# Head-pair scan of a hybrid RWKV-7 / PEER layer: score products over zero-padded 128-row operands, two PSUM banks for scores, and one barrier between passes

## The reference, cut to what matters

```python
def step(s, xs):                      # s: state [value, key] of one head
    r_t, w_t, k_t, v_t, kk_t, a_t = xs
    sa = jnp.einsum('bhvk,bhk->bhv', s, -kk_t)
    s = (s * w_t[:, :, None, :] + sa[..., None] * (kk_t * a_t)[:, :, None, :]
         + v_t[..., None] * k_t[:, :, None, :])
    y = jnp.einsum('bhvk,bhk->bhv', s, r_t)
```

## Time and profile before

| what | us |
| --- | --- |
| median of 3 runs | 3511.05 |
| lowest, highest | 3495.39, 3520.24 |
| profiled execution, its own time | 3520.24 |
| its span in the profile | 3518.1 |
| the scan's block, 808.5 to 1381.7 | 573.2 |
| mean granted TensorE clock in the scan | 0.95 |

### The profile page before, as it was taken

How to read it: one execution, slowest core, us unless ns; L and a number is a source line. 1 busy time by engine, 2 the same in 40 slices (tenths; PEclk the granted TensorE clock), 3 DMA queues, 4 the chain that set the end, 5 groups by cost and what they waited for, 6 DMA issues and landing times.

```text
span 3518.1 us, 58248 instructions
## 1 busy us (share of the span) xinstructions
PE 3053.6 (87%) x22248; PEld 2615.1 (74%) x22248; DVE 2436.1 (69%) x3113; ACT 1434.1 (41%) x1827; POOL 726.0 (21%) x386
## 2 busy tenths in 40 slices
PE   6987998967888887696997877699999799999997
PEld 2336998955666665685997877699999687787776
DVE  5995553247555655535998877577777698999997
ACT  6884332323333334225333555433333243333333
POOL 0000000001010001103664322111111234444442
PEclk9998999987999999898998988899999899999998
DMA  9992332300000000223445888899999999999996
GB/s 378 421 406 108 120 130 106 122 23 5 8 5 5 5 7 26 83 84 147 141 153 194 299 300 300 292 346 358 360 359 356 402 418 417 417 417 417 417 417 258
DMA packets 207434, 811.63 MB, mean 231 GB/s; under 512 B 81472, under 2 KB 101056, under 8 KB 118336
## 3 DMA queue, kind: packets, MB, share of 16 engines
q1 hardware_dynamic: 170432, 541.14, 41.4%
q0 software_dynamic: 36864, 268.45, 19.1%
HBM read 769.16 MB, written 40.37 MB: 230 GB/s over the span
## 4 chain that ended last, share of the span: by engine, by line
DMA 27%; PE 11%; DVE 9%; ACT 4%; issue 3%; SPq 1%; POOL 1%; DVEq 0%; ACTq 0%
DMA work<-act_table 12%; DMA raw<-expert_u 11%; DMA x<-u_rows,idx 3%; DVE wlo L2076 2%; ACT whi L1733 2%; DVE x L2034 2%; DVE wlo L2116 2%; PE ps L1538 1%; PE ps L1539 1%; PE ps L1540 1%; PE ps L1795 1%; PE ps L1796 1%; PE ps L1797 1%; DVE wlo L1527 1%; DVE work L2111 1%
## 5 line engine op out<-in xcount | busy, mean ns | idle before, releaser
L1538 PE MATMUL ps<-hhi,whi 128*128 128x256 f32 x2048 | 595.9, 291 | 68.8 <-DVE wlo L1527 31.5
L1539 PE MATMUL ps<-hlo,whi 128*128 128x256 f32 x2048 | 584.8, 286 | 0.0
L1540 PE MATMUL ps<-hhi,wlo 128*128 128x256 f32 x2048 | 584.4, 285 | 0.0
L1538 PEld LDWEIGHTS ps<-hhi,whi 128*128 128x128 f32 x2048 | 398.5, 195 | 83.5 <-issue 34.8
L1888 PE MATMUL ps<-whi,hhi 128*128 128x512 f32 x1024 | 402.9, 393 | 34.7 <-DVE hlo L2094 18.4
L282 PE MATMUL ps<-hhi,whi 128*128 128x384 f32 x1056 | 357.5, 339 | 79.0 <-DVE hlo L1395 42.8
L1889 PE MATMUL ps<-wlo,hhi 128*128 128x512 f32 x1024 | 400.1, 391 | 0.0
L1890 PE MATMUL ps<-whi,hlo 128*128 128x512 f32 x1024 | 399.8, 390 | 0.0
L1539 PEld LDWEIGHTS ps<-hlo,whi 128*128 128x128 f32 x2048 | 398.8, 195 | 0.0
L1540 PEld LDWEIGHTS ps<-hhi,wlo 128*128 128x128 f32 x2048 | 398.2, 194 | 0.0
L1921 POOL DMA_INDIRECT work<-expert_v,idx x128 | 296.3, 2315 | 432.3 <-DVE work L2111 414.6
(11 more groups left out here) (295 smaller groups left out, 5957.6 us busy)
## 6 DMA issues: line engine op xcount, KB each, us to landing
raw<-expert_u SPq DMA_DIRECT2D x128, 1024.0 KB, 7.8
z<-w_ada SPq DMA_DIRECT2D x72, 1024.0 KB, 15.4
raw<-expert_v SPq DMA_DIRECT2D x64, 1024.0 KB, 15.0
work<-expert_v SPq DMA_DIRECT2D x64, 1024.0 KB, 13.2
raw<-w_in SPq DMA_DIRECT2D x50, 1024.0 KB, 4.8
raw<-w_ada SPq DMA_DIRECT2D x24, 1024.0 KB, 14.2
raw<-w_out SPq DMA_DIRECT2D x16, 1024.0 KB, 4.8
raw<-w_query SPq DMA_DIRECT2D x16, 1024.0 KB, 5.0
```

What stands on the lines that cost most here:

```text
L1538: pe.matmul(bank, whi[:, r, k, :], moving_hi, start=(k == 0), stop=False)
L1539: pe.matmul(bank, whi[:, r, k, :], moving_lo, start=False, stop=False)
L1540: last = pe.matmul(bank, wlo[:, r, k, :], moving_hi, start=False, stop=(k == KD - 1))
```

## The change

It makes four edits.

- The two heads of a pair no longer share TensorE's rows. A buffer `alone`, laid over the eight columns of `z` from `Z_VG` on (free by then), holds for each operand, direction and head a full 128-partition copy in which the other head's 64 partitions are zero. GpSimd clears it once, in a block of its own ahead of the scan. ScalarE fills the live halves with four copies for each direction (`front_alone`), for the next pass after its copies n = 16 and n = 21 of the inverse. The score products contract over all 128 rows of `alone` and `kr`, and a score is two matmuls.
- The scores go by group and tile in turn and use banks 6 and 7 alone, so a score waits for the mask two before it.
- GpSimd's group `g` waits for 3(g + 1) masks.
- `y_copied`, `state_stored` and the waits at the end of a pass give way to a barrier, `pass_done`: each of the five engines adds one at the end of a pass (the compute engines after a drain) and waits at the start of the next for all five. GpSimd's copy of v stands behind it.

```diff
--- before.py
+++ after.py
@@ -740,6 +740,11 @@
+        with nc.Block() as block:
+            @block.gpsimd
+            def _(pool):
+                nc.gpsimd.memset(z[:, Z_VG:Z_VG + HB, :], 0.0)
@@ -774,6 +779,7 @@
+            alone = z[:, Z_VG:Z_VG + 8, :].rearrange("p (b d h) t -> p b d h t", b=2, d=2)
             kr = [buf(f"kr{d}", [P, TILES, 2, P]) for d in range(2)]
@@ -797,11 +803,11 @@
-            y_copied, state_stored = sem("y_copied"), sem("state_stored")
+            pass_done = sem("pass_done", 1)
             lora_landed, state_landed = sem("lora_landed"), sem("state_landed")
...
             centred, factors = signal("centred", 2), signal("factors", 2)
-            multiplied = signal("multiplied", 4)
+            multiplied, alone_ready = signal("multiplied", 4), signal("alone_ready", 2)
             halves, operands = signal("halves", 2), signal("operands", 2)
@@ -839,6 +845,15 @@
+            ENGINES = 5
+            def begin(eng, it):
+                eng.wait_ge(pass_done.sem, it * ENGINES + 1)
+            def end(eng):
+                eng.drain().then_inc(pass_done.sem, 1)
@@ -847,6 +862,7 @@
                 def one(it, front):
+                    begin(sp, it)
                     sp.dma_start(s_in[:, :, :], state_t[bass.ds(it, 1)].rearrange("o p a c -> (o p) a c")
@@ -856,9 +872,10 @@
                     sp.wait_ge(stores.sem, it * 16 + stores.v + 16)
-                    sp.sem_inc(state_stored.sem, 1)
+                    sp.sem_inc(pass_done.sem, 1)
                 load_lora(0)
+                sp.sem_inc(pass_done.sem, 1)
                 with sp.Fori(0, PAIRS - 1) as it:
@@ -866,17 +883,18 @@
                 with pool.Fori(0, PAIRS) as it:
+                    begin(pool, it)
                     v_copied.inc(nc.gpsimd.tensor_copy(vs[:, :], zb(Z_V, it)))
...
                         d = g // 2
-                        scores_masked.wait(pool, it, 2 * TILES * d + 2 * TILES - 1 + g % 2)
+                        scores_masked.wait(pool, it, TILES * (g + 1))
                         m = scan_tables(f"two{d}").to_broadcast([P, TILES, P])
...
                     ch.close(PAIRS)
-                    bonus_used.wait(pool, it, 1)
+                    end(pool)
@@ -895,7 +913,16 @@
+                def front_alone(it, d):
+                    for b, src in enumerate((bq[d], kq[d])):
+                        multiplied.wait(act, it, 2 * d + b + 1)
+                        for hh in range(2):
+                            last = nc.scalar.activation(alone[heads[hh], b, d, hh, :], src[heads[hh], :], ACT.Copy)
+                    alone_ready.inc(last)
                 def one(it, more):
+                    begin(act, it)
@@ -918,6 +945,8 @@
                                 front_factors(it + 1, n // 4 - 1)
+                            elif n in (16, 21):
+                                front_alone(it + 1, (n - 16) // 5)
                     for turn, w in ((0, 2), (2, 1)):
@@ -928,10 +957,10 @@
                     y_sum.wait(act, it, 1)
-                    nc.scalar.activation(zb(Z_R, it), ps[:, 5, 0:T], ACT.Copy).then_inc(y_copied.sem, 1)
-                act.sem_inc(y_copied.sem, 1)
-                for step in (front_gates, front_factors):
+                    nc.scalar.activation(zb(Z_R, it), ps[:, 5, 0:T], ACT.Copy)
+                    end(act)
+                for step in (front_gates, front_factors, front_alone):
                     for d in range(2):
@@ -988,6 +1017,7 @@
                 def one(it, more):
+                    begin(dve, it)
                     ch = Chain(dve, dve_chain, it, 7)
@@ -1005,10 +1035,10 @@
                     for n in range(12):
-                        d, tile, g = n // (2 * TILES), n // 2 % TILES, 2 * (n // (2 * TILES)) + n % 2
+                        g, tile = n // TILES, n % TILES
                         scores.wait(dve, it, n + 1)
-                        scores_masked.inc(nc.vector.tensor_tensor(G[:, g, tile], ps[:, 4 + n % 4, :].rearrange("p (a t) -> p a t", a=4),
-                                                                  scan_tables(f"ab{d}", 4), ALU.mult))
+                        scores_masked.inc(nc.vector.tensor_tensor(G[:, g, tile], ps[:, 6 + n % 2, :].rearrange("p (a t) -> p a t", a=4),
+                                                                  scan_tables(f"ab{g // 2}", 4), ALU.mult))
@@ -1049,8 +1079,7 @@
                                                                   in1=table("head_sum"), op0=ALU.mult, op1=ALU.mult))
-                    dve.wait_ge(state_stored.sem, it + 1)
-                    y_sum.wait(dve, it, 1)
+                    end(dve)
@@ -1071,6 +1100,7 @@
                 def one(it, more):
+                    begin(pe, it)
                     for d in range(2):
@@ -1083,22 +1113,18 @@
                     gates.wait(pe, it, 4)
-                    for n in range(2 * TILES):
-                        d, tile = n // TILES, n % TILES
+                    for n in range(12):
+                        g, tile = n // TILES, n % TILES
+                        d, hh = g // 2, g % 2
                         c = slice(tile * P, (tile + 1) * P)
-                        if tile == 0:
+                        if n % 6 == 0:
                             operands.wait(pe, it, d + 1)
-                        if n == 0:
-                            pe.wait_ge(y_copied.sem, it + 1)
+                            alone_ready.wait(pe, it, d + 1)
                         if n >= 2:
-                            scores_masked.wait(pe, it, 2 * n - 2)
-                        for b, src in enumerate((bq, kq)):
-                            for hh in range(2):
-                                m = kr[d][heads[hh], tile, :, :].rearrange("p a t -> p (a t)")
-                                last = pe.matmul(ps[:, 4 + 2 * (n % 2) + hh, b * 2 * P:(b + 1) * 2 * P], src[d][heads[hh], c], m,
-                                                 start=True, stop=True)
-                                if b:
-                                    scores.inc(last)
+                            scores_masked.wait(pe, it, n - 1)
+                        m = kr[d][:, tile, :, :].rearrange("p a t -> p (a t)")
+                        pe.matmul(ps[:, 6 + n % 2, 0:2 * P], alone[:, 0, d, hh, c], m, start=True, stop=True)
+                        scores.inc(pe.matmul(ps[:, 6 + n % 2, 2 * P:4 * P], alone[:, 1, d, hh, c], m, start=True, stop=True))
                     bonus_in.wait(pe, it, 1)
@@ -1214,6 +1240,7 @@
                     y_sum.inc(last_y[0])
+                    end(pe)
```

More of the change, by code:

```diff
@@ L819, in build_program @@
             y_sum = signal("y_sum", 1)
-            every = [v_copied, gates_in, gates, centred, factors, multiplied, halves, operands, bonus_in,
+            every = [v_copied, gates_in, gates, centred, factors, multiplied, alone_ready, halves, operands, bonus_in,
                      bonus_sum, bonus_used, scores, scores_masked, init_ready, turned, tn_ready, xs_, xm, tps, tadds, tt_turned,
```

## The result

| what | before | after |
| --- | --- | --- |
| median of 20 runs each, us | 3518.88 | 3538.98 |
| lowest, highest | 3490.94, 3531.1 | 3518.43, 3556.74 |
| profiled execution's span | 3518.1 | 3541.1 |
| scan, from VectorE's last product ahead of it to the start of the last copy of y | 572.9 | 606.7 |

The ratio is 1.0062, with a 95% interval of 1.0042 to 1.0082: 15 to 29 us more. The predicted 3537 lies 2 us from the measured median and the forecast of "within 1%" held. But the scan itself grew by 33.7 us (before rounding), where the prediction's sum says 26.4, and the sum's terms were off in both directions. The hit is better than its reasons.

A forecast was written before the change was run, and what follows sets the result against it. The scan was taken as a chain between engines, DMA at 2%. Terms 13.2 + 6.0 + 2.1 + 3.6 + 1.5 = 26.4 us on the profiled 3520.2 gave 3546.6, lying 9.2 above the median, hence 3537; range 3510 to 3568.

The forecast's parts named there:

- scores: Score products in each pass: 0.95 us a score, bound by TensorE, adding 1.65 us a pass, 13.2 us over eight.
- ScalarE's copies: Inverse of seven passes: two sets of four copies, 1.75 us each, delay TensorE by 0.85 us a pass, 6.0 together.
- barrier's gap: End of a pass: only the drain shows, 0.3 us at each of seven boundaries, 2.1 us.
- memset and block: Ahead of the scan: 3.1 us of clearing plus 0.5 us of seam, 3.6 us once.
- clock: Scan: number of half-clock stretches unchanged, each costing 0.3 us more in five passes, 1.5 us.
- The other bound of the prediction: Two-bank handover in the scores: 0.63 us of mask, 0.2 to start it, 0.1 to be seen, 0.93 us.
- Rival 3: Scores: masks stay the bound, 15 us gained against 3.6 + 6.0 + 2.1 paid, 3508 us; chance 0.05.
- the slack that I took off: Inverse: slack shortens the delay from ScalarE's second set of copies, so TensorE gets the right-hand sides about 0.4 us late.
- The bound of 1.1 us: Pass boundary: upper end of the barrier's cost, from TensorE's end to the release, if the gap starts only after it.
- Rival 1: Pass boundaries: the gap grows and the clock falls in it, nine stretches of 1.7 us, 3558 us; chance 0.22.
- Rival 2: Passes of the scan: fuller scores keep the clock up, 15 us less, 3522 us; chance 0.20.
- The undisturbed pass: A pass at full clock: 68.3 + 1.65 + 0.85 + 0.3 = 71.1 us.

The follow-up runs named there:

- e1: The kernel after with the barrier taken out and the old waits put back; ratio 1.0054 to the kernel before, scan 589.3 us.
- e2: The kernel before with the barrier in place of its waits and nothing else changed; ratio 1.0051 to the kernel before, scan 589.9 us.
- e4: The kernel after with TensorE reporting to the barrier without a drain; ratio 1.0065 to the kernel before, scan 602.5 us.
- e10: The kernel after with TensorE's looped passes written out, barrier and drain kept; ratio 1.0050 to the kernel before, scan 585.8 us.
- e9: The kernel after with unpadded 64-row scores, no copies or memset, and old waits for the barrier; ratio 1.0156 to the kernel before, scan 632.4 us.
- after again: The kernel after, unchanged, profiled a second time; scan 606.3 us.
- e6: The kernel after with the copies into alone moved from ScalarE to GpSimd; ratio 1.0038 to the kernel before, scan 604.3 us.
- e7: The kernel before with TensorE's looped passes written out; ratio 1.0002 to the kernel before, scan 576.4 us.
- e11: The kernel before with passes written out, unread filler products and earlier TensorE waits for ScalarE's copies; ratio 0.9975 to the kernel before, scan 563.7 us.
- e3: The kernel after with unpadded 64-row scores, no copies or memset, barrier kept; ratio 1.0217 to the kernel before, scan 657.6 us.

## Why the prediction was right, and where it was not

| term | predicted | measured |
| --- | --- | --- |
| scores | 1.65 x 8 = 13.2 | 2.1 x 8 = 16.8 |
| ScalarE's copies | 0.85 x 7 = 6.0 | 1.55 x 7 = 10.9 |
| barrier's gap | 0.3 x 7 = 2.1 | 1.4 x 6, and 0.5 once: 8.9 |
| memset and block | 3.6 | 3.0 |
| clock | +1.5 | 33.7 less the above: -5.9 |
| scan | 26.4 | 33.7 |

**The scores.** The size of a step held, 0.957 us a score against 0.95, and GpSimd ends at S+14.45 in e1. The mechanism held in part. The prediction let TensorE win with 0.86 us of products and "0.09 for the semaphore wait that every score now has". The instructions of a score do start 0.216 us apart, 0.86 for four; but what is added is a wait for the mask two back, in which both engines wait in turn: 0.76 us from the first to the fourth instruction, 0.42 to the start of the mask, 0.69 of mask and 0.05 to the next score in that bank are 1.92 us for two scores. The other bound of the prediction, the handover at 0.93, left TensorE's instructions out and took 0.63 for the mask. That 0.95 came out is partly luck. More than two banks should bring a score nearer to the 0.86 of its instructions, an estimate from their pitch; no kernel here has padded scores in more. The term is 0.45 too small because it ended with GpSimd. Behind that TensorE's last transposes still stand behind a ScalarE copy and a product of the next pass's gates, and the inverse's first mask comes 2.1 us later. Rival 3, that the masks set the pace by themselves, is out: there is a gap ahead of each. The page TensorEngine Tiling of the Trainium skill (PSUM Bottleneck), which spoke for it, is right in part here: 0.957 us a score stands against 0.69 us of mask, but the mask is in the round trip.

**ScalarE.** The failed step is the duration, taken from operations that start 0.41 us apart. These copies start 0.53 us apart, 2.14 us a set and not 1.75; the slack that I took off was right in size, so nearly all the difference of 0.4 us a set reached TensorE.

**The barrier.** The failed step is "what shows is the drain ... I take 0.3 us". The bound of 1.1 us named beside it, "if the gap starts only after it", was the better reading, and even this was exceeded: 1.4 us on average, 1.5 in e2. The loading of instructions that TensorE waits for starts 1.0 to 1.7 us behind the copy of y instead of with it. The wait for the others costs little in the loop (0.3 us, e4 against e1), nearly as said; e10 has it at 0.6 us where the jump is gone.

**The clock.** "I leave the number of stretches as it is" failed. Both rivals of this were half right. Rival 1: all six boundaries of the loop have a stretch at half clock now, where five had (four in the second trace of before); but one, not two, and they cost 1.7 us each. Rival 2: the stretches inside the passes (13.7 us in it=2, 6.8 and 3.4 in the first and the last) are gone, as it expected of fuller scores. Together 40.9 us at half clock became 23.8, where I had charged 1.5 us more. At 1.7 us for each 3.4 that would give back 8.5; the table's remainder is 5.9, since the longest stretches cost less than that rate (in it=2 of before, 17.1 us at half cost 6.9). So the three costs that were too low, by 3.6, 4.9 and 6.8 us, were in part made up for by a clock that I had with the wrong sign; that is luck. That padded scores keep the clock is shown by e1, which has 3.4 us at half clock with before's waits, against e9, the same without padding, with 126.3.

**The median.** The forecast was +0.74% on the three runs' 3511.05; twenty runs put before at 3518.88 and the change at +0.62%. The 3537 came so close because the base was 8 us low and the effect 6 us high. Against 20.1 us between the medians (15 to 29 by the interval), the scan gained 33.7. Part of the rest may lie in the `expert_u` loads: the five traces of kernels with both padded scores and the barrier (after, after again, e4, e6, e10) had them at 1099.0, 1080.7, 1083.8, 1077.9 and 1097.7 us, mean 1087.8, the eight others at 1078.0 to 1122.6, mean 1103.4. Whether that is chance, or a scan that ends later meets those reads otherwise, stays open. The undisturbed pass was forecast at 71.1 us; no pass of the kernel after is undisturbed, and e1's 72.0 with the gap's 1.4 would make 73.4.

## What to carry to other kernels

Ask of TensorE's idle places what they do to its clock before asking what they cost themselves: a gap taken away (e4, e7) was paid back by a longer stretch at half clock, and products that nobody reads (e11) made a pass shorter. Where products of 64 rows can't be paired, try padding them to 128 rows: unpadded passes took 82.0 us and padded ones 75.1, copies and all, though at full clock an unpadded pass was the shorter by 1 us (70.9, e9). Pairs in four banks are better still, by 3.7 us a pass at full clock. When two engines wait for each other in turn, as in these scores, add up the round trip of a bank; the busy time of either engine is too little. And look at TensorE's jump back in a long loop, and at the packets of instructions beside it: with passes written out the wait is gone, and a drain ahead of the jump puts the loading off.

## What the hardware showed that I had not expected

- TensorE comes round a loop of 905 matmul instructions in 2.3 to 2.8 us, and in 3.7 to 4.3 with a drain ahead of the jump; written out, the same place takes 0.1 and 0.6 us. A 16 KB packet of instructions is loaded at each jump, in 0.88 to 1.40 us, and the first transpose comes 1.5 to 1.8 us behind its end.
- The granted clock was not the same for 64-row and padded scores: at the same count of these instructions and the same columns, 64-row scores alone had it at 0.50 for 27.3 us of every pass it=1 to it=6 (e3); with padding to 128 rows it was 1.00 after 3.4 us in most.
- ScalarE's copies of 64 partitions by 384 columns follow each other every 0.53 us, exponentials of 128 by 384 every 0.41.
- GpSimd clears 3072 columns in 2.66 us, 0.87 ns a column, where short memsets gave 1.0 ns.
- Two executions of one kernel differ by 35 us in one stretch, in which `expert_u` is read.
